# Accumulating a 31-tap causal convolution in two PSUM banks instead of two SBUF rows

## The reference

```python
a = _causal_dwconv(a_u * jax.nn.sigmoid(a_v), conv_a_w[l]) + conv_a_b[l]   # 31 taps, 512 channels
a = jax.nn.silu(_layer_norm(a, ln_a_g[l], ln_a_b[l]))
y_a = (a * jax.nn.silu(a_gate)) @ p_a[l]
```

## Time and profile before

| | |
|---|---|
| median of 3 runs | 1318.26 us (1317.86 to 1320.16) |
| profiled execution | 1321.32 us |
| its span | 1319.5 us |
| mean granted clock of TensorE | 0.98 |
| TensorE busy | 1234.6 us (94%) |
| GpSimd busy | 769.4 us (58%) |
| VectorE busy | 886.0 us (67%) |
| ScalarE busy | 545.4 us (41%) |

### The profile page before, as it was taken

One profiled execution on the slowest core, in us unless ns is written; L12 is line 12 of the kernel. 1 busy time (PEld: TensorE's weight loads), 2 busy tenths in 40 slices (PEclk: granted clock), 3 DMA queues, 4 the chain that ended last, 5 costly groups with the idle time before them and its releaser, 6 DMA issues.

```text
span 1319.5 us, 16434 instructions
## 1 busy us (share of the span) xinstructions
PE 1234.6 (94%) x5704; PEld 1009.8 (77%) x5704; DVE 886.0 (67%) x1199; ACT 545.4 (41%) x1000; POOL 769.4 (58%) x528
## 2 busy tenths in 40 slices
PE   6799999999999999999999999999998889899997
PEld 4588788777777777788888878778787777678886
DVE  4615876797697796427777666767667466766864
ACT  4443333332423433557335555645545334314200
POOL 6888989999999999878503132132321224446200
PEclk8799999998999999999999999999999999999999
DMA  6121221222222223323602111111002423247332
GB/s 193 55 62 44 64 72 57 64 97 96 98 94 96 96 98 119 104 97 96 223 2 81 49 49 48 32 48 48 24 10 89 164 97 107 92 152 275 98 126 80
DMA packets 92132, 118.49 MB, mean 90 GB/s; under 512 B 5912, under 2 KB 73496, under 8 KB 92064
## 3 DMA queue, kind: packets, MB, share of 16 engines
q1 hardware_dynamic: 92064, 117.60, 27.2%
HBM read 92.39 MB, written 25.20 MB: 89 GB/s over the span
## 4 chain that ended last, share of the span: by engine, by line
PE 45%; POOL 25%; DVE 9%; issue 5%; ACT 3%; DMA 0%; DVEq 0%; ACTq 0%; POOLq 0%; SPq 0%
POOL ring_lo L1476 15%; POOL w_pair L1504 7%; PE pj L734 4%; PE pj L735 4%; PE pj L736 4%; PE pj L982 3%; PE pj L751 3%; PE pj L753 2%; PE pj L752 2%; PE pj L695 2%; PE pj L697 2%; PE pj L696 2%; POOL s_w L1504 2%; PE po L843 2%; PE pt L830 2%
## 5 line engine op out<-in xcount | busy, mean ns | idle before, releaser
L1476 POOL TENSOR_TENSOR ring_lo<-w_pair,ring_hi 128x512 fp32r<-128x512 f32 x180 | 310.7, 1740 | 43.9 <-ACT ring_hi L1040 43.8
L1685 DVE SCALAR_TENSOR_TENSOR slot<-glu,cwa,slot 128x1024 f32<-128x1024 f32 x116 | 234.1, 2054 | 24.5 <-ACT slot L1092 24.5
L1545 POOL TENSOR_TENSOR w_lo<-w_raw,w_hi 128x128 fp32r<-128x128 f32 (+1 forms) x104 | 107.3, 1051 | 243.5 <-ACT w_hi L1135 241.3
L1040 ACT ACTIVATE ring_hi<-w_pair 128x512 fp32r<-128x512 f32 x180 | 110.5, 626 | 225.4 <-POOL w_pair L1504 178.4
L695 PE MATMUL pj<-t_hi,ring_hi 128*128 128x512 f32 x420 | 168.5, 401 | 25.4 <-POOL ring_lo L1476 10.7
L696 PE MATMUL pj<-t_lo,ring_hi 128*128 128x512 f32 x420 | 166.5, 396 | 0.0
L697 PE MATMUL pj<-t_hi,ring_lo 128*128 128x512 f32 x420 | 166.4, 396 | 0.0
L734 PE MATMUL pj<-xT_hi,w_hi 128*128 128x512 f32 x320 | 126.4, 395 | 0.0
L735 PE MATMUL pj<-xT_lo,w_hi 128*128 128x512 f32 x320 | 125.4, 392 | 0.0
L736 PE MATMUL pj<-xT_hi,w_lo 128*128 128x512 f32 x320 | 125.0, 391 | 0.0
L695 PEld LDWEIGHTS pj<-t_hi,ring_hi 128*128 128x128 f32 x420 | 80.6, 192 | 49.7 <-issue 12.7
(11 more groups left out here) (273 smaller groups left out, 2927.2 us busy)
## 6 DMA issues: line engine op xcount, KB each, us to landing
w_pair<-in_w_in SPq DMA_DIRECT2D x28, 1024.0 KB, 5.2
gate_scratch<-slot SPq DMA_DIRECT2D x16, 1024.0 KB, 4.0
gate<-gate_scratch SPq DMA_DIRECT2D x32, 512.0 KB, 3.6
w_raw<-in_w_in SPq DMA_DIRECT2D x20, 512.0 KB, 3.9
z_scratch<-slot SPq DMA_DIRECT2D x8, 512.0 KB, 2.7
bias<-cum_scratch SPq DMA_DIRECT2D x8, 512.0 KB, 3.7
wout_raw<-in_w_out SPq DMA_DIRECT2D x8, 512.0 KB, 5.8
x_tok<-in_x SPq DMA_DIRECT2D x8, 512.0 KB, 4.4
```

The lines of the kernel that those rows point to most:

```text
L1040: nc.scalar.activation(ring_hi[:, j % RING, :, :], w_src(u, p), ACT.Copy).then_inc(s_rhi, 1)
L1476: nc.gpsimd.tensor_tensor(ring_lo[:, j % RING, :, :], w_src(u, p), ring_hi[:, j % RING, :, :], ALU.subtract).then_inc(s_rlo, 1)
L1545: nc.gpsimd.tensor_tensor(w_lo[:, j % 2, k, :], w_raw[:, j % 2, k, :], w_hi[:, j % 2, k, :], ALU.subtract).then_inc(s_wlo, 1)
L1685: nc.vector.scalar_tensor_tensor(out=acc, in0=glu[:, ct, n:n + T], scalar=cwa[:, ct, n:n + 1], in1=acc, op0=ALU.mult, op1=ALU.add).then_in ...
```

## The change

Each tile is accumulated in the two banks of `po`: one bank for the first 512 tokens, one for the last 512. ScalarE makes tap 0 alone, with the bias, in two operations of 128x512. VectorE makes taps 1 to 30, each in two operations of 128x512, one a bank. The last tap reads the bank and writes to `glu` in place, second half first, so there is no closing addition. A tile then has 60 operations on VectorE instead of 30, and the counts of `CONV_UNITS` and of the waits on `s_conv` are doubled. Places in the queues stay.

```diff
@@ -103,10 +103,11 @@
 
     CONV_UNITS, at = {}, 0
     for u in range(4, AG0 - 4):
-        count = (4, 4, 4, 4, 4, 4, 3, 3, 8, 8, 7, 7, 8, 8, 7, 7, 8, 8, 7, 7)[u - 4]
+        count = (8, 8, 8, 8, 8, 8, 6, 6, 16, 16, 14, 14, 16, 16, 14, 14, 16, 16, 14, 14)[u - 4]
         CONV_UNITS[u] = (at, count)
         at += count
-    assert at == 30 * CT
+    CONV_OPS = 2 * (CONV_A - 1)
+    assert at == CONV_OPS * CT
 
     ADD_NO, ADDM_NO = {}, {}
     for s, (br, dt) in TILE.items():
@@ -520,7 +521,7 @@
                     sp.dma_start(g_dram[2 * i:2 * i + 2, :, :].rearrange("n p t -> p n t"),
                                  slot[u % 2][:, :, :]).then_inc(s_gst[u % 2], 16)
                 if u == AG0 - 2:
-                    sp.wait_ge(s_conv, 30 * CT)
+                    sp.wait_ge(s_conv, CONV_OPS * CT)
                     sp.dma_start(wf_raw[:, :, :], w_in[:, col["f"]:col["f"] + HEADS].rearrange("(k p) c -> p k c", p=P)
                                  ).then_inc(s_wf, 16)
                     for t, src in ((memg[:, :], mem_ln_g), (memb[:, :], mem_ln_b),
@@ -1086,17 +1087,14 @@
                 act.wait_ge(s_glu, 4)
                 act.wait_ge(s_xfree[1], 2)
                 if ct:
-                    act.wait_ge(s_conv, 30 * ct)
-                else:
-                    act.wait_ge(s_xbl, 8)
-                nc.scalar.activation(slot[2][:, 0, :], glu[:, ct, 0:T], ACT.Identity, scale=cwa[:, ct, 0:1],
-                                     bias=cab[:, ct:ct + 1]).then_inc(s_conv0, 1)
-                nc.scalar.activation(slot[2][:, 1, :], glu[:, ct, 1:1 + T], ACT.Identity,
-                                     scale=cwa[:, ct, 1:2]).then_inc(s_conv0, 1)
+                    act.wait_ge(s_conv, CONV_OPS * ct)
+                for h in range(2):
+                    nc.scalar.activation(po[:, h, :], glu[:, ct, h * HALF:(h + 1) * HALF], ACT.Identity,
+                                         scale=cwa[:, ct, 0:1], bias=cab[:, ct:ct + 1]).then_inc(s_conv0, 1)
 
             def mean_hi(ct):
 
-                act.wait_ge(s_conv, 30 * (CT if ct == 0 else CT))
+                act.wait_ge(s_conv, CONV_OPS * CT)
                 if ct >= 2:
                     act.wait_ge(s_lmm, ct - 1)
                 else:
@@ -1675,19 +1673,17 @@
 
             def conv_op(ct, k):
 
-                acc = slot[2][:, k % 2, :]
-                if k < CONV_A - 2:
-                    n = k + 2
-                    if k < 2:
-                        dve.wait_ge(s_conv0, 2 * ct + k + 1)
-                    else:
-                        dve.wait_ge(s_conv, 30 * ct + k - 1)
-                    nc.vector.scalar_tensor_tensor(out=acc, in0=glu[:, ct, n:n + T], scalar=cwa[:, ct, n:n + 1], in1=acc,
-                                                   op0=ALU.mult, op1=ALU.add).then_inc(s_conv, 1)
+                n, h = 1 + k // 2, k % 2 if k < CONV_OPS - 2 else 1 - k % 2
+                acc = po[:, h, :]
+                src = glu[:, ct, n + h * HALF:n + (h + 1) * HALF]
+                if k < 2:
+                    dve.wait_ge(s_conv0, 2 * ct + h + 1)
+                elif k < CONV_OPS - 2:
+                    dve.wait_ge(s_conv, CONV_OPS * ct + k - 1)
                 else:
-                    dve.wait_ge(s_conv, 30 * ct + k)
-                    nc.vector.tensor_tensor(glu[:, ct, PAD_A:WA], slot[2][:, 0, :], slot[2][:, 1, :],
-                                            ALU.add).then_inc(s_conv, 1)
+                    dve.wait_ge(s_conv, CONV_OPS * ct + k)
+                nc.vector.scalar_tensor_tensor(out=acc if n < PAD_A else src, in0=src, scalar=cwa[:, ct, n:n + 1], in1=acc,
+                                               op0=ALU.mult, op1=ALU.add).then_inc(s_conv, 1)
 
             def silu_gate(u, part):
 
@@ -1817,7 +1813,7 @@
                     if u in CONV_UNITS:
                         first, count = CONV_UNITS[u]
                         for n in range(first + count * i // 7, first + count * (i + 1) // 7):
-                            conv_op(n // 30, n % 30)
+                            conv_op(n // CONV_OPS, n % CONV_OPS)
 
                     if (u, i) in ((AG0 - 4, 1), (AG0 - 4, 5)):
                         for ct in (i // 2, i // 2 + 1):
```

## The result

The changed kernel takes **1283.86 us** (median of 4 runs, 1283.24 to 1286.53), against 1318.06 us for the kernel before (4 runs). The ratio is 0.9743, with a 95% interval of 0.9724 to 0.9763: 34.2 us faster, where 34.4 us were forecast. The profiled execution took 1283.24 us with a span of 1281.5 us.

What follows compares the result with a forecast made beforehand. VectorE and GpSimd, slowing each other over SBUF, were taken to hold TensorE back: 35.6 - 0.7 - 0.5 = 34.4 us gained, 1318.26 - 34.4 = 1283.9, 1284 us. Range 1279 to 1299; forecast case 1279 to 1290, chance 0.75.

Steps and rivals of the forecast that it cites:

- 35.6 us are lost in the stage: Projection stage, 160 to 540 us: 1520 matmuls need 344.4 of 380 us at full pace; 35.6 us is all that can be won.
- Two SBUF inputs on VectorE and GpSimd's reads hold each other up: Convolution beside GpSimd: VectorE operations reading two SBUF tensors conflict with GpSimd; 2.27 us for a GpSimd operation against 1.30.
- The new operation at 0.65 us: VectorE's multiply-add with output in PSUM: 0.65 us each, 240 taking 156 us, between bounds of 0.60 and 1.27 us.
- 688 ns row: Nearest profiled VectorE operation to the new one: same opcode, 128x512, in1 in PSUM, 688 ns.
- GpSimd at 1.30 us: GpSimd's 11 operations a unit fall from about 1.74 to 1.30 us, 14.3 us a unit, under TensorE's 19.04 us.
- ScalarE's halves at about 0.6 us: First tap on ScalarE: 8 operations of about 0.6 us instead of 8 x 1.2, worth nothing on the end.
- 0.7 and 0.5 us stay at the short convolution and the LayerNorm: Losses that remain: 0.7 us around the short convolution's two-SBUF taps, 0.5 us before the LayerNorm's matrix steps.
- The 9.4 us of waits for VectorE: TensorE's waits for VectorE's sums before the change: VectorE needed 3.0 us per product, more than the 2.72 us between products.
- Rival B: New operation still holds GpSimd's reads; units take 22.3 us instead of 21.0, 16 us slower, 1334 us; chance 0.05.

Runs made afterwards that it cites:

- one_tap: Changed kernel with taps 1 to 29 left out, so VectorE does two operations a tile instead of 60: 1281.85 us.
- halves_in_sbuf: Changed kernel with the same 240 half-length operations in the same places, but the accumulators in SBUF instead of PSUM: 1334.93 us.
- load_half: Changed kernel plus 112 VectorE operations of 128x512 with one SBUF and one PSUM input, results unread: 1287.04 us.
- load_half_two_sbuf: Changed kernel plus 112 unread VectorE operations of 128x512, placed as in load_half but with both inputs in SBUF: 1300.76 us.
- gpsimd_load: Changed kernel plus 5 unread GpSimd operations of 128x512 in each of units 8 to 23, 80 in all: 1300.52 us.
- load_full: Changed kernel plus 216 VectorE operations with one PSUM input, one behind nearly every convolution operation: 1308.74 us.
- run 240: Not a run's label: in "Over the whole run 240 short ones" the number counts the half-length operations of halves_in_sbuf, which took 1334.93 us.

## Why the prediction was right

The time was forecast at 1284 us and measured at 1283.86. Its steps one by one:

- *35.6 us are lost in the stage, and no more can be won there.* Right: from unit 4 on 35.8 us were won, one_tap found nothing more, and TensorE is without a gap.
- *Two SBUF inputs on VectorE and GpSimd's reads hold each other up; with one in PSUM they don't.* Right, and shown by two pairs: the changed kernel against halves_in_sbuf, which differ in the home of the accumulator (an input and the output of the operation), and load_half against load_half_two_sbuf, which differ in one input alone. The per-partition scalar in SBUF doesn't count as an input. By the Trainium skill's page "SBUF — State Buffer", section Who interferes with whom, the new operation should be free of the conflict, and the trace agrees: 1.29 to 1.30 us for GpSimd's splits beside such operations.
- *The new operation at 0.65 us.* Its row says 749 ns and it follows at 0.66 us. 240 x 0.66 = 158 us: right. The 688 ns row was for an output in SBUF, and the prediction's doubt was the output in PSUM. That home costs nothing: the last tap of each tile reads the same and writes to `glu` in SBUF, and takes as long, 748 ns in the middle by the line's own view (below). What the 688 ns row has otherwise is its scalar, a constant instead of a value per partition; so has the added operation of load_half, at 677 ns. That the scalar makes the 0.06 us is the difference left between them, not tried by itself. By the Trainium skill's page "VectorE: DVE Perf Modes", in its section on the TRN2 errata, the fixed cost depends on where an operation reads. The trace agrees in so far as the output's home changes nothing.

```profile
L1685 DVE SCALAR_TENSOR_TENSOR glu<-glu,cwa,po x8: 736/748/751, 261.0 to 487.1; 128x512 f32<-128x512 f32 x8
```

- *GpSimd at 1.30 us.* 1.29 to 1.30 alone; the splits' mean over the whole run is 1.44 us, since operations with two SBUF inputs are left on VectorE, in the gating and the other convolution; that these cause it is read from their inputs, not tested. It didn't matter at 155 of 210 us.
- *ScalarE's halves at about 0.6 us.* Too low: 774 ns in the middle, by the line's own view (ns least, median, most). Without effect, as the sum said.

```profile
L1092 ACT ACTIVATE po<-glu,cab,cwa x8: 769/774/777, 112.6 to 418.0; 128x512 f32<-128x512 f32 x8
```

- *0.7 and 0.5 us stay at the short convolution and the LayerNorm.* Wrong in size: nothing stayed; from 160 to 540 us TensorE waits for neither, and the whole 35.8 us came back. These 1.2 us, a run-to-run spread of 3 us and the 1.8 us behind the stage are of one size, so the hit within 0.2 us is partly luck.
- *The 9.4 us of waits for VectorE come from 3.0 us of work per product against 2.72.* Half right. load_half has more VectorE time than before the change and loses 3 us. What made VectorE late at those five places of the kernel before was not tried by itself.
- *Rival B, 1334 us, from 10 such waits a unit on.* It didn't come about for the changed kernel, but where it applies, in halves_in_sbuf, its sum came out, with two terms off that nearly cancel. It stays the best argument for the accumulator's place: halves without PSUM are worse than either.

One number goes most of the way: the longest of three lengths of a unit, TensorE's 19.04 us, GpSimd's operations and VectorE's queue. It is 21.0 (GpSimd) in the kernel before and the unit measured 21.4; 19.04 (TensorE) and 19.0 in the changed kernel; 19.7 (GpSimd) and 19.6 in gpsimd_load. Where VectorE is the longest, its busy time alone falls short: 20.2 us against 21.1 in load_full, 19.2 against 20.7 in load_half_two_sbuf, 20.9 against 22.9 in halves_in_sbuf. Its waits at the heads of the tiles and for TensorE's products belong to its queue too; how much each adds was not taken apart.

## What to carry to other kernels

Where GpSimd and VectorE both stream through SBUF and TensorE waits for either, look for VectorE operations with two SBUF tensor inputs and give one of the inputs a home in a free PSUM bank; the gain is bounded by counting matmuls in the stretch against their pitch, and it stops where TensorE's pace begins. Don't cut two-input SBUF operations into shorter ones: each one can pay the conflict anew. Compare engines by the length of their work in one unit, waits at fixed places included: the longest sets the pace, and the others' load was nearly free up to that (3 us in load_half).

## What the runs showed of the hardware that I had not expected

- A two-input SBUF operation of 128x512 takes 1275 ns in the mean beside a busy GpSimd (halves_in_sbuf, 200 to 500 us), its full-length sister 2054 ns: half the work for 62% of the time. Over the whole run 240 short ones keep VectorE busy for 306 us, 116 long ones for 234 us.
- A multiply-add of 128x512 with one input in PSUM takes 748 ns with its output in PSUM and 748 ns with its output in SBUF, when the scalar is a value per partition; with a constant in its place it takes 677 ns (to SBUF). A single 128x1024 operation over two banks takes 1285 ns.
- ScalarE pays for such an operand too. In the kernel before, its second first-tap operation has the scale per partition but no bias, and takes 1140 ns against the 1232 ns of the one with both the earlier trace rows:

```profile
L1094 ACT ACTIVATE slot<-glu,cwa 128x1024 f32<-128x1024 f32 x4 | 4.6, 1140 | 0.0
```

- GpSimd adds a 128x512 tensor to itself in 1084 ns (the added operations of gpsimd_load), and two different ones in 1.30 us.
